# Lists of the first four experts made directly from positions, table behind the first expert, shared down product in six halves

## The reference

```
xn     = rmsnorm(x) * (1 + sc_f) + sh_f
scores = sigmoid(xn @ router_w)
idx    = top_k(scores + bias, 8);  gates = 2.5 * scores[idx] / sum(scores[idx])
routed = sum over e of gates[:, e] * ((silu(xn @ Wg[e]) * (xn @ Wu[e])) @ Wd[e])
shared = (silu(xn @ Sg) * (xn @ Su)) @ Sd
y      = rmsnorm(x + g_f * (routed + shared)) * final_norm_g
```

## Time and profile before

| | |
|---|---|
| median of three runs | 824.01 us (819.41, 824.01, 829.22) |
| profiled execution | 825.24 us, span 823.5 us |
| TensorE busy | 702.2 us, 85% |
| VectorE, ScalarE, POOL busy | 320.5, 230.6, 305.3 us |
| DMA, whole span | 279.18 MB, mean 339 GB/s |
| granted TensorE clock, mean | 0.956 |

### The profile page before, as it was taken

How to read it: one execution, slowest core, us unless ns; L and a number is a source line. 1 busy time by engine, 2 the same in 40 slices (tenths; PEclk the granted TensorE clock), 3 DMA queues, 4 the chain that set the end, 5 groups by cost and what they waited for, 6 DMA issues and landing times.

```text
span 823.5 us, 14501 instructions
## 1 busy us (share of the span) xinstructions
PE 702.2 (85%) x4895; PEld 391.2 (48%) x4896; DVE 320.5 (39%) x582; ACT 230.6 (28%) x391; POOL 305.3 (37%) x318
## 2 busy tenths in 40 slices
PE   3599999999899979999889979998789987997830
PEld 1167656346545535554445536554355443544510
DVE  3006375556603463234232331433423434233217
ACT  4112632023223422233222321332322323232212
POOL 5001012021333554456452553555436444354230
PEclk9889999999899989999999999999999999999985
DMA  9989999609546999999999999999999999999643
GB/s 275 373 289 313 297 383 335 222 30 394 194 145 249 389 405 415 396 384 382 396 387 391 397 393 405 402 394 398 405 414 402 401 404 403 402 400 403 270 111 111
DMA packets 74659, 279.18 MB, mean 339 GB/s; under 512 B 19039, under 2 KB 22235, under 8 KB 48880
## 3 DMA queue, kind: packets, MB, share of 16 engines
q1 hardware_dynamic: 50082, 252.00, 76.8%
q0 software_dynamic: 23264, 26.07, 13.2%
q10 hardware_dynamic: 1262, 0.43, 0.3%
HBM read 272.28 MB, written 26.04 MB: 362 GB/s over the span
## 4 chain that ended last, share of the span: by engine, by line
PE 57%; DMA 33%; DVE 4%; issue 3%; SPq 1%; ACT 1%; POOL 0%; POOLq 0%; DVEq 0%
DMA gu<-in_exp_w_up 28%; PE bank L1078 23%; PE bank L1114 9%; PE bank L831 5%; PE bank L840 4%; DMA gu<-in_ada_w 4%; PE bank L958 3%; PE bank L1063 2%; PE bank L806 2%; PE bank L1163 1%; PE bank L1095 1%; DMA sh<-acc_rows 1%; PE bank L843 1%; PE bank L964 1%; PE bank L1041 1%
## 5 line engine op out<-in xcount | busy, mean ns | idle before, releaser
L1078 PE MATMUL bank<-gu,et 128*64 128x256 f32 x2496 | 289.9, 388 | 42.3 <-DMA gu<-in_exp_w_up 36.2
L1078 PEld LDWEIGHTS bank<-gu,et 128*64 128x64 f32 x2496 | 184.3, 140 | 168.7 <-issue 93.5
L505 POOL DMA_INDIRECT acc_rows<-et,idx x64 | 104.6, 1634 | 271.7 <-DVE et L1574 185.6
L1114 PE MATMUL bank<-dn,et 128*64 128x512 f32 x624 | 149.8, 608 | 15.8 <-issue 13.6
L1565 DVE COPY et<-bank 128x256 f32<-128x256 f32 x64 | 27.1, 424 | 271.3 <-PE bank L1095 268.4
L712 ACT ACTIVATE et<-bank 64x512 f32<-64x512 f32 x64 | 37.9, 592 | 268.7 <-PE bank L1078 268.7
L1114 PEld LDWEIGHTS bank<-dn,et 128*64 128x64 f32 x624 | 40.4, 137 | 82.1 <-issue 82.1
L723 ACT ACTIVATE et<-bank,mb 128x512 f32<-128x512 f32 x64 | 44.0, 687 | 122.3 <-PE bank L1114 110.5
L1574 DVE TENSOR_SCALAR et<-bank,mb 128x512 f32<-128x512 f32 x64 | 48.0, 751 | 69.1 <-PE bank L1114 61.3
L1558 DVE TENSOR_TENSOR et<-et 64x512 f32<-64x512 f32 x64 | 67.8, 1060 | 0.4 <-ACT et L713 0.4
L515 POOL DMA_DIRECT2D small<-halfc x50 | 57.3, 1147 | 0.0
(11 more groups left out here) (279 smaller groups left out, 606.2 us busy)
## 6 DMA issues: line engine op xcount, KB each, us to landing
gu<-in_exp_w_gate SPq DMA_DIRECT2D x64, 1024.0 KB, 21.8
gu<-in_exp_w_up SPq DMA_DIRECT2D x64, 1024.0 KB, 27.2
dn<-in_exp_w_down SPq DMA_DIRECT2D x64, 1024.0 KB, 27.4
gu<-in_ada_w SPq DMA_DIRECT2D x12, 2048.0 KB, 15.6
gu<-in_w_in SPq DMA_DIRECT2D x3, 2048.0 KB, 18.5
gu<-in_w_out SPq DMA_DIRECT2D x2, 2048.0 KB, 17.2
acc_rows<-gn SPq DMA_DIRECT2D x2, 1280.0 KB, 16.9
gu<-in_w_in SPq DMA_DIRECT2D x2, 1024.0 KB, 19.6
```

What stands on the lines that cost most here:

```text
L505: pool.indirect_dma_start(acc_rows[u % 2], bass.IndirectOffsetOnAxis(ap=idx[:, u, 0:1], axis=0), yo[:, u % 2, 0, :], None, bounds_check=2 ...
L1078: mm = pe.matmul(bank[u % 2][64 * c:64 * c + 64, b * FE:(b + 1) * FE], xt[:, b, k % 4, k // 4, :], w[:, (c * KT + k) * FE:(c * KT + k + 1) ...
L1114: mm = pe.matmul(bank[5 + b][64 * c:64 * c + 64, :], hT[:, b, j, :], dn[:, dslot(u), j * D + c * HALF:j * D + (c + 1) * HALF], start=(j == ...
```

## The change

`FIRST` = 4 experts get their lists by a way of their own: `first_lists` (VectorE) compares the position column of each of them with the row of places, for three tiles at once, and `lists` (TensorE) multiplies these one-hots by two columns (token number and gate) for each, in the middle of the shared product of tile 2. `spread_first` (ScalarE) copies the result to `tt`, and index and gather of experts 0 to 3 follow from it. The table of all experts is made in batches of 3, 3 and 2 ranks; its products stand behind gate_up(0) (the first two batches) and behind turn_x(1) (the last). VectorE's one-hots come behind the first indices, POOL's `moving` behind the first three gathers. The index of expert 4 waits for the whole table.

The shared down product is made in six halves (3 tiles x 2 column halves), one behind each of down(1) to down(6), that is in the turns u = 2 to 7 of the first group. Transposes, product and the multiplication by gmod all stand in bank 7, from which VectorE adds to x. Its weights move to `sh`, loaded when the table's products are through; the first four `dn` slots so go to experts 0 to 3. The final norm's row is loaded last of SP's transfers before the end.

```diff
@@ -45,6 +45,7 @@
+FIRST = 4
@@ -151,7 +152,7 @@
-        shid = et[:, o[0] - 768:o[0]].rearrange("p (t f) -> p t f", t=3)
+        shid = gn[:, 0:3 * FE].rearrange("p (t f) -> p t f", t=3)
...
-        KH = TOP // 2
+        BATCHES = ((0, 3), (3, 6), (6, 8))
+        xTf = xT[:, :, :].rearrange("p k t -> p (k t)")
...
-        mv = et[:, 2048:5120].rearrange("p (k t e c) -> p k t e c", k=TOP, t=3, c=2)
+        mvd = mbf[:, 3160:3160 + 6 * FIRST].rearrange("p (t e c) -> p t e c", t=3, c=2)
+        prod = xnf[:, 2 * D + FE:2 * D + FE + 576].rearrange("p (k t e) -> p k t e", k=3, t=3)
+        mv = xTf[:, 0:2304].rearrange("p (b k t e c) -> p b k t e c", b=2, k=3, t=3, c=2)
         oh = shf.rearrange("p (k t n) -> p k t n", k=TOP, t=3)
+        ohd = oh[:, TOP - FIRST:TOP]
+        shw = shf[:, 0:2 * D]
         tt = mbf[:, 3840:4096].rearrange("p (e b c) -> p e b c", b=2, c=2)
 
@@ -315,8 +320,6 @@
-            sync.wait_ge(s["acc_zeroed"], 32)
-            sync.dma_start(gn[:, :], io["final_norm_g"].rearrange("(o n) -> o n", o=1).to_broadcast([P, D])).then_inc(s["gn_fin"], 16)
@@ -347,21 +348,23 @@
                 load_gu(0, 0, u)
             sync.wait_ge(s["ya_done"], CT)
             sync.wait_ge(s["mix_free"], 1)
-            sync.dma_start(dn[:, 0, :], io["shared_w_down"][0].rearrange("(p j) n -> p (j n)", j=2)).then_inc(ld_shared_dn, 16)
-            for u in range(2):
+            for u in range(3):
                 load_dn(0, 0, u)
             load_gu(0, 0, 3)
-            load_dn(0, 0, 2)
+            load_dn(0, 0, 3)
             load_gu(0, 0, 4)
+            sync.wait_ge(s["tb_mm"], TOP)
+            sync.dma_start(shw, io["shared_w_down"][0].rearrange("(p j) n -> p (j n)", j=2)).then_inc(ld_shared_dn, 16)
             for u in range(5, U):
                 load_gu(0, 0, u)
-                load_dn(0, 0, u - 2)
-            load_dn(0, 0, U - 2)
+                load_dn(0, 0, u - 1)
...
             load_dn(0, NE // U - 1, U - 1)
+            sync.wait_ge(s["h_ready"], 3)
+            sync.dma_start(gn[:, :], io["final_norm_g"].rearrange("(o n) -> o n", o=1).to_broadcast([P, D])).then_inc(s["gn_fin"], 16)
...
-                for h in range(2):
-                    pool.wait_ge(s["mk_done"], 2 * r + h + 1)
-                    pool.tensor_tensor(mv[:, KH * h:KH * h + KH, :, :, 1], mk[:, KH * h:KH * h + KH], over_k(gpart), ALU.mult).then_inc(s["mv_gate"], 1)
+            def moving(r, h):
+                a, b = BATCHES[h]
+                pool.wait_ge(s["mk_done"], 3 * r + h + 1)
+                if h == 0 and r == 0:
+                    pool.wait_ge(s["sh_ready"], 3)
+                if h == 2:
+                    pool.wait_ge(s["tb_mm"], TOP * r + 3)
+                pool.tensor_tensor(mv[:, h % 2, 0:b - a, :, :, 1], mk[:, a:b], over_k(gpart, b - a), ALU.mult).then_inc(s["mv_gate"], 1)
 
...
             def rounds(r):
-                moving(r)
-                if r == 0:
+                if r:
+                    for h in range(3):
+                        moving(r, h)
+                else:
                     pool.wait_ge(s["flags"], 1)
                     pool.wait_ge(s["tok_written"], 48)
                     pool.wait_ge(s["xg_zero"], 1)
                     pool.wait_ge(s["acc_zeroed"], 32)
                 for u in range(AHEAD):
                     gather(r, 0, u)
+                if r == 0:
+                    moving(0, 0)
+                    moving(0, 1)
...
+            def spread_first():
+                act.wait_ge(s["dl_mm"], FIRST)
+                for b in range(2):
+                    for h in range(2):
+                        act.activation(tt[64 * h:64 * h + 64, 0:FIRST, b, :],
+                                       bank[7][64 * b:64 * b + 64, 256:256 + 2 * FIRST].rearrange("p (e c) -> p e c", c=2),
+                                       ACT.Copy).then_inc(s["tt_done"], 1)
...
+                    spread_first()
                     shared_act(1)
-                moving_tokens(r, 1)
-                if r == 0:
+                    moving_tokens(0, 0)
...
+            def lists():
+                pe.wait_ge(s["route_step"], 15)
+                pe.wait_ge(s["sc_done"], 3)
+                for e in range(FIRST):
+                    pe.wait_ge(s["ohd_done"], e + 1)
+                    for t, (t0, m) in enumerate(TILES):
+                        mm = pe.matmul(bank[7][:, 256 + 2 * e:258 + 2 * e], ohd[0:m, e, t, :], mvd[0:m, t, e, :], start=(t == 0), stop=(t == 2))
+                    mm.then_inc(s["dl_mm"], 1)
                     gate_up(r, i, u, now)
+                    now_shared = first and r == 0 and u >= U - 6
                     if first and r == 0 and u == 0:
-                        shared_down(1)
-                        shared_down(2)
+                        table(0, 0)
+                        table(0, 1)
                     if before is not None:
                         turn_h(r, i if u else i - 1, (u - 1) % U, before)
+                    if now_shared and u % 2 == 0:
+                        shared_turn((u - U + 6) // 2)
                     after = None
                     if not (last and u == U - 1):
                         after = is_full(r, i + (u + 1) // U, (u + 1) % U)
                         turn_x(r, i + (u + 1) // U, (u + 1) % U, after)
+                    if first and r == 0 and u == 0:
+                        table(0, 2)
                     if before is not None:
                         down(r, i if u else i - 1, (u - 1) % U, before)
+                    if now_shared:
+                        shared_down(u - U + 6)
...
+                for j in range(2):
+                    mm = pe.matmul(bank[7][0:n, :], shT[:, j, 0:n], shw[:, j * D + c * HALF:j * D + (c + 1) * HALF], start=(j == 0), stop=(j == 1))
+                mm.then_inc(s["sh_down_ready"], 1)
...
+                    tile_product(bank[6], 2, gu[SH_SLOT], 2 * FE, range(4))
+                    lists()
+                    tile_product(bank[6], 2, gu[SH_SLOT], 2 * FE, range(4, KT)).then_inc(s["sh_ready"], 1)
                     pe.wait_ge(s["flags"], 1)
...
+            def shared_sum(m):
+                t, c = m // 2, m % 2
+                n = TILES[t][1]
+                y, cols = bank[7][0:n, :], slice(c * HALF, (c + 1) * HALF)
+                if m == 0:
+                    dve.wait_ge(s["gf_in"], 32)
+                dve.wait_ge(s["sh_down_ready"], m + 1)
+                link(dve.tensor_tensor(y, y, gmod[0:n, t // 2, cols], ALU.mult))
+                dve.tensor_tensor(x[0:n, t, cols], x[0:n, t, cols], y, ALU.add).then_inc(s["pre_done"], 1)
+
+            def first_lists():
+                dve.wait_ge(s["out_small"], 64)
+                dve.tensor_tensor(mvd[:, :, :, 0], mask[:, :, 0:FIRST], over_e(tokc[:, :], FIRST), ALU.mult).then_inc(s["route_step"], 1)
+                dve.tensor_copy(mvd[:, :, :, 1], gpart[:, :, 0:FIRST]).then_inc(s["route_step"], 1)
+                for e in range(FIRST):
+                    dve.tensor_tensor(ohd[:, e], iota_s[:, 0:P].rearrange("p (o n) -> p o n", o=1).to_broadcast([P, 3, P]),
+                                      pos[:, :, e:e + 1].to_broadcast([P, 3, P]), ALU.is_equal).then_inc(s["ohd_done"], 1)
-                    if not (last and u >= U - AHEAD - 1):
+                    now_shared = first and r == 0 and u >= U - 6
+                    if now_shared and u % 2 == 0:
+                        shared_turned((u - U + 6) // 2)
+                    late = first and r == 0 and u == 0
+                    if not (late or last and u >= U - AHEAD - 1):
                         index(r, i + (u + AHEAD + 1) // U, (u + AHEAD + 1) % U)
-                    if first and r == 0 and u == 0:
-                        shared_turned(1)
-                        shared_turned(2)
                     if not (last and u == U - 1):
                         xt0(r, i + (u + 1) // U, (u + 1) % U)
                     hidden(r, i, u)
+                    if late:
+                        index(r, 0, FIRST)
                     if not (first and u == 0):
                         y0(*before)
+                    if now_shared:
+                        shared_sum(u - U + 6)
 
             def rounds(r):
                 if r == 0:
                     dve.wait_ge(s["iota_in"], 1)
-                one_hots(r, 0)
                 if r == 0:
+                    first_lists()
                     counts()
+                    for u in range(AHEAD + 1):
+                        index(0, 0, u)
                     shared_hidden(0)
-                one_hots(r, 1)
-                if r == 0:
+                    one_hots(0, 0)
                     shared_hidden(1)
+                    one_hots(0, 1)
+                    xt0(0, 0, 0)
                     shared_hidden(2)
-                for u in range(AHEAD + 1):
-                    index(r, 0, u)
-                if r == 0:
-                    shared_turned(0)
-                xt0(r, 0, 0)
```

(70 more changed lines are left out.)

119 lines of the change are left out of this document (58 added, 61 removed).

## The result

The changed kernel took 845.55 us as the median of four runs (844.29 to 848.57), the kernel before beside it 822.32 (819.41 to 829.22, four runs): a ratio of 1.0257, 95% interval 1.0217 to 1.0296. The forecast was 818, range 811 to 827. The profiled run of after took 848.57 us at a span of 846.8.

The account below looks back on a forecast made before the run. The prediction took TensorE to lead up to the routing and weight transfers to the end; 4.0 us of path plus 2.6 of transfers gave 6.6, the backlog allowed 6.3, so 825.2 became 818.9, as a median about 818, range 811 to 827.

Parts of the forecast that it names:

- Two things decide the end: Weight transfers: expert 5's load issue with the MB behind it, and the backlog up to expert 17, limit the gain.
- The slower rival: Bank 7 makes TensorE wait before each shared half; over 1% slower (832 us) from 4.6 us per half; chance 10%.
- The way through the hole: From routing past the DMA lull at 220 to 230 us: gate_up(1) ends at 248.6 instead of 252.6.
- the old stall behind the first group: Behind expert 12: VectorE's six multiply-adds, 7.3 us, no longer delay TensorE; expert 13's slot is freed at 316.8.
- quick gather: Expert 0's first tokens there at 219.9, gate_up(0) starting at 225.4: 815 to 817 us; chance 22%.
- the rule of turns between queues: DMA engines alternate between queues by packet, so the first gather waits behind at most one weight piece.
- free lists: The 24 list passes take next to nothing, all behind them up to 3.8 us earlier: 814 us; chance 5%.
- the estimate of 0.6 us for all 24: List passes at about 25 ns each without weight load: all behind them 3.2 us earlier, 815 instead of 818.
- costly halves: Shared down halves cost more than 2.2 us each: 824 us at 3.2 each, 827 at 3.7; chance 9%.
- the second limit: The transfer backlog must survive TensorE's slow stretch up to expert 17; it allows 6.3 us of gain.
- 4.0 of path: gate_up(1) ends at 248.6 instead of 252.6, and expert 5's load waits for it: 4.0 us.
- 2.6 of transfers: At expert 5's issue 60 down weights remain, not 61, as 1 MB moves into the hole: 2.6 us.

Follow-up runs that it names:

- e1: The changed kernel with 140 idle TensorE instructions ahead of TensorE's first product: 822.84 us, ratio 0.9985 to before.
- e3: The kernel before with 54 idle TensorE instructions ahead of TensorE's first product, no work changed: 843.11 us, ratio 1.0197 to before.
- e8: The kernel before with 12 idle TensorE instructions ahead of TensorE's first product: 826.79 us in one run.
- e9: The kernel before with 24 idle TensorE instructions ahead of TensorE's first product: 826.35 us in one run.
- e11: The kernel before with 36 idle TensorE instructions at its start: 842.49 us, ratio 1.0199 to before.
- e10: e1 with expert 3's weights issued only once expert 0's tokens are there, and these tokens copied before the second one-hots: 818.59 us, ratio 0.9912 to before.
- e6: e5 with expert 3's weights issued only when expert 0's tokens are there: ratio 0.9990, no faster than e5.
- e7: e6 with both copies of expert 0's tokens ahead of the second batch of one-hots: ratio 0.9995, no faster than e5.
- e5: The changed kernel with 112 idle TensorE instructions between tile 2's shared product and the first transposes: 822.97 us, ratio 0.9986 to before.
- e4: The kernel before with 256 idle TensorE instructions ahead of TensorE's first product: 829.09 us, ratio 1.0027 to before.

## Why the prediction was wrong

**The step that failed** is the premise under the sum, "Two things decide the end": when expert 5's load is issued with how many MB behind it, and whether the backlog survives up to expert 17. TensorE's later turns of the loop were so put at no change, without a reason. What the runs showed in its place is a third thing: TensorE stands 8.6 to 10.9 us at each of five returns of the loop, 48.6 us in all, and the end is then set by TensorE and no longer by the transfers (33% of the chain before, 8% after). The added TensorE instructions, the 24 passes of the lists above all, were costed by duration (3.8 us; measured 3.5 to 4.3). That they also move all code behind them was not costed, not named as a rival, and the q8 row of the page was not read. The slower rival (10%, 832 us) named another mechanism, bank 7: e1 has the same use of the bank and is not slower, so that a slower case stood among the chances earns the forecast nothing.

This case's q8 rows and the stalls at the loop's return show that TensorE's instructions are fetched again there: the row names no engine, but e3 differs from before by idle TensorE instructions alone, and its packets go from 31 to 76. From 380 to 720 us q8 moves no packet in before and 42 in after. The Trainium skill (Runtime: NRT & Kernel Launch, Instruction fetch mechanics) says that instructions come in blocks of 256, that TensorE holds 128 KiB, and that a jump whose target is outside the current window of two pages forces a fetch before execution goes on. On the standstill the traces agree in kind. On the window they don't: in before a jump back over more than six blocks finds its code six turns long without a packet, so most of the eight blocks of the 128 KiB are kept. At which length or place they no longer are, the page does not say, and e8, e9 and e11 do not settle it.

By its own steps, read from e1, the changed kernel without the stalls:

| step | forecast | e1 |
|---|---|---|
| 24 list passes | 3.8 | 3.46 |
| indices of expert 0 | 214.5 | 213.27 |
| first transposes | 223.8 | 224.37 |
| gate_up(0) | 226.6, 9.0 long | 227.31, 9.14 long |
| gate_up(1) ends | 248.6 | 248.9 |
| turn of experts 2 to 7 | 9.0 | (299.66 - 248.94)/6 = 8.45 |
| slots of experts 12 and 13 free | 310.0, 316.8 | 307.86, 314.44 |
| slot of expert 17 free | 3.4 later than before | 1.1 later (354.77) |

The way through the hole was right to about a microsecond (by a little luck: routing stood 0.7 us early in e1), the halves were cheaper (1.8 with everything, not 2.2: the gate issues of experts 6 and 12 lie 50.7 us apart, 40.0 in before, 10.8 for six halves), and the old stall behind the first group went as said. The rivals of the prediction did not occur: no quick gather while expert 3's weights go beside it (7.20 and 8.18 us, against 2.75 without them, so the estimate by the rule of turns between queues does not come out here), no free lists (0.14 to 0.18 us per short pass with its weight load, so the forecast's 0.16 stands and the estimate of 0.6 us for all 24 does not come out), no costly halves. I could not read expert 17's landing, as the trace of e1 pairs none; its DMA share is 1.01 or more in every window from 250 to 600, so the second limit seems not to have bound.

The size of the gain was off too. 4.0 of path and 2.6 of transfers should give 6.6. The path's part, counted from the count products, was 48.5 - 45.6 = 2.9 in e1, the remaining 0.7 of the 3.7 being a routing that happened to be early. Between single profiles e1 gained 5.5 us of span (818.0 against 823.5); between medians 2.7, and the ratio allows 3.7 at most. The 140 idle instructions are not seen to cost any of it (65.76 against 66.54 above). What took the rest of the 6.6 stays open; e10, in which the gather and the copies of expert 0's tokens are quicker, does gain more.

**Open.** Where exactly the edge lies, and why with 12 and with 24 instructions three of five returns are fetched anew. And the start of the out-projection at 145 us: TensorE stood 4.14 us there in after and then computed at a slower clock, 16.32 us for products that took 13.97 before. In the other kernels (before and e1 to e11) it stood 0.5 to 2.7 and took 13.97 or 15.6 to 15.7, with no order that follows the edits. It makes most of the 5.9 us by which after's routing is late, and no experiment was made on it.

## What to carry to other kernels

Where an engine runs a loop whose code is near what it can hold, count its instructions and their place before costing an edit ahead of it, and read the instruction queue's packets and the "issue" pieces at the loop's return in both profiles; if they rise, shift the code by idle instructions, and judge the edit by that version. A stall can be hidden in waits that the engine has anyway: here three cost nothing that one run each could show, and five cost 2%. And put filler where no one waits for the engine, and measure how long it lasts: what hides under one latency becomes the bound when you remove it.

## What the runs showed of the hardware

- The loop's code: 9 packets for a stalled return, some 16.5 KB each, and 8 to 11 us of standstill (8.18 in e11 to 11.45 in e3), with TensorE's granted clock at 0.63 over the first one in after (380 to 390).
- A gather of 64 rows took 2.75 us with no weights beside it (e6; 2.76 in e7) and 7.20 and 8.18 with three 1 MB transfers issued beside it (e5, e1).
- An idle TensorE instruction (a satisfied wait) took 0.089 us (22.68 us for 256 in e4).
- VectorE's one-hots of two operands from SBUF took 1.50 us for three, and 4.81 when POOL multiplied at the same time (227.54 and 228.19 in after). The Trainium skill (SBUF — State Buffer, SBUF: two separate sides) gives a shared pair of ports that one of the two holds for its whole instruction; 4.81 is 1.50 plus 3.31, the 2.79 of POOL's two instructions and 0.5 more.
